# Attention units taken two at a time on the tensor engine, with a third buffer for the turned probabilities

## The reference

```
# even: 12 query heads of 64, 4 key heads, blocks of 128 queries, window of 128 to each side, a sink
p = exp(scores * HEAD_DIM**-0.5 - max);  out = p / (sum(p) + exp(sink - max)) @ v
# mix2: grouped: 8 query heads, 2 key heads, all 512 keys;  latent: 8 heads, keys of 64 + 32 (rotary), 512 keys
def one_block(qblk):                      # 128 queries
    sc = jnp.einsum('bqhgd,bkhd->bhgqk', qblk, k) * scale
    p = jax.nn.softmax(sc, axis=-1)
    return jnp.einsum('bhgqk,bkhd->bqhgd', p, v)
```

## Time and profile before

| | |
|---|---|
| time, median of 3 runs | 3439.11 us |
| span of the profiled execution | 3440.3 us |
| PE busy | 3396.7 us, 99% |
| DVE, POOL, ACT busy | 2088.8, 1993.6, 1529.6 us |
| attention of even | 440.2 to 506.9 us |
| attention of the first mix2 | 2074.9 to 2196.6 us |
| attention of the second mix2 | until 2927.3 us |

### The profile page before, as it was taken

One profiled execution on the slowest core, in us unless ns is written; L12 is line 12 of the kernel. 1 busy time (PEld: TensorE's weight loads), 2 busy tenths in 40 slices (PEclk: granted clock), 3 DMA queues, 4 the chain that ended last, 5 costly groups with the idle time before them and its releaser, 6 DMA issues.

```text
span 3440.3 us, 46280 instructions
## 1 busy us (share of the span) xinstructions
PE 3396.7 (99%) x17556; PEld 2760.0 (80%) x17556; DVE 2088.8 (61%) x2990; ACT 1529.6 (44%) x2388; POOL 1993.6 (58%) x2338
## 2 busy tenths in 40 slices
PE   9999999999999999999999999999999999999999
PEld 8888868888888888748888887788788877888887
DVE  5556766554764468766645657326766575238667
ACT  4334454333633354675333537434444545335444
POOL 6555655555655658735665557554655655546564
PEclk9999999999999999999999999999999999999999
DMA  4223303233222323202333220133222210232331
GB/s 173 93 75 115 110 18 123 74 110 111 88 97 96 125 71 94 69 1 83 123 111 107 79 75 26 50 98 123 98 98 88 90 59 8 92 104 92 115 107 62
DMA packets 89262, 303.59 MB, mean 88 GB/s; under 512 B 10448, under 2 KB 15056, under 8 KB 88656
## 3 DMA queue, kind: packets, MB, share of 16 engines
q1 hardware_dynamic: 86928, 298.53, 25.9%
q10 hardware_dynamic: 2112, 2.10, 0.2%
HBM read 296.39 MB, written 2.10 MB: 87 GB/s over the span
## 4 chain that ended last, share of the span: by engine, by line
PE 50%; DVE 5%; POOL 2%; issue 1%; ACT 1%; DMA 0%; DVEq 0%; POOLq 0%; ACTq 0%
PE bank L421 9%; PE bank L422 9%; PE bank L423 9%; PE bank L978 3%; PE bank L979 3%; PE bank L980 3%; PE bank L1295 2%; PE bank L1272 2%; PE scores L1257 2%; POOL extra_lo L410 2%; PE bank L2376 1%; PE bank L2377 1%; PE bank L2378 1%; DVE sqsum L579 1%; PE bank L1756 1%
## 5 line engine op out<-in xcount | busy, mean ns | idle before, releaser
L410 POOL TENSOR_TENSOR w_lo<-w_raw,w_hi 128x256 fp32r<-128x256 f32 x1754 | 1369.0, 814 | 1085.2 <-ACT w_hi L383 835.8
L421 PE MATMUL bank<-xh,w_hi 128*128 128x512 f32 x2544 | 997.0, 392 | 4.0 <-issue 1.5
L423 PE MATMUL bank<-xh,w_lo 128*128 128x512 f32 x2544 | 989.9, 389 | 0.0
L422 PE MATMUL bank<-xl,w_hi 128*128 128x512 f32 x2544 | 989.7, 389 | 0.0
L383 ACT ACTIVATE w_hi<-w_raw 128x1024 fp32r<-128x1024 f32 (+2 forms) x485 | 498.6, 1039 | 671.2 <-DMA w_raw<-in_ffn_up 269.4
L421 PEld LDWEIGHTS bank<-xh,w_hi 128*128 128x128 f32 x2544 | 478.5, 188 | 105.8 <-issue 4.1
L423 PEld LDWEIGHTS bank<-xh,w_lo 128*128 128x128 f32 x2544 | 478.3, 188 | 99.9
L422 PEld LDWEIGHTS bank<-xl,w_hi 128*128 128x128 f32 x2544 | 478.7, 188 | 98.0 <-issue 1.4
L410 POOL TENSOR_TENSOR extra_lo<-extra_raw,w_hi 128x256 fp32r<-128x256 f32 x264 | 229.7, 905 | 126.3 <-ACT w_hi L383 113.2
L1101 DVE TENSOR_TENSOR y_tok<-y_tok,bank 128x512 f32<-128x512 f32 x232 | 157.2, 684 | 223.1 <-PE bank L980 223.1
L1135 DVE TENSOR_TENSOR work<-bank,sqsum 128x512 f32<-128x512 f32 x88 | 60.6, 689 | 269.7 <-PE bank L423 269.7
(11 more groups left out here) (452 smaller groups left out, 6145.6 us busy)
## 6 DMA issues: line engine op xcount, KB each, us to landing
w_raw<-in_ffn_up SPq DMA_DIRECT2D x176, 512.0 KB, 3.5
w_raw<-in_b_ffn_up SPq DMA_DIRECT2D x64, 512.0 KB, 3.6
extra_raw<-in_ffn_down SPq DMA_DIRECT2D x52, 512.0 KB, 4.6
w_raw<-in_b_gates SPq DMA_DIRECT2D x48, 512.0 KB, 3.4
extra_raw<-in_b_ffn_down SPq DMA_DIRECT2D x40, 512.0 KB, 4.7
w_raw<-in_od_in SPq DMA_DIRECT2D x33, 512.0 KB, 3.7
w_raw<-in_b_in SPq DMA_DIRECT2D x24, 512.0 KB, 4.0
w_raw<-in_ffn_down SPq DMA_DIRECT2D x20, 512.0 KB, 3.4
```

The source lines that it names most:

```text
L410: ins = pool.tensor_tensor(lo_of(g, part), raw_of(g, part), hi_of(g, part).bitcast(F32), ALU.subtract)
L421: pe.matmul(out, wh, hi, start=first, stop=False)
L422: pe.matmul(out, wh, lo, start=False, stop=False)
L423: return pe.matmul(out, wl, hi, start=False, stop=last)
```

## The change

PE takes two units per step. Step k is: score(2k), score(2k+1), turn(2k-3), value(2k-5), value(2k-4), turn(2k-2). A joint now stands directly behind the passes of its own unit. The last value product of a call stands behind the second fill. `turned` has a third buffer, `turned_c`, laid over memory that is unused at that time, so the copies wait for the value product of unit g-3 and not g-2.

ACT takes per step: copy a(2k-3), exponentials(2k) and (2k+1) with their guests, copy a(2k-2), then the hi of 2k-5 or 2k-4. DVE keeps one unit per loop turn: maximum(s), reciprocal(s-1), then lo(s-7) (before: lo(s-5), behind the copy), then copy b(s-3). POOL, the DMA and the work of every station are unchanged.

```diff
-            for s in range(n + BEHIND + 1):
-                ...
+            for k in range(n // 2 + 3):
+                for s in (2 * k, 2 * k + 1):
+                    if s in early:
+                        early[s]()
+                    if s < n:
+                        score(s)
+                if 2 * k in fill:
+                    pe.wait_ge(probs_ready, c.units + n)
+                    fill[2 * k]()
+                if 0 <= 2 * k - 3 < n:
+                    turn(2 * k - 3)
+                if 0 <= 2 * k - 5 < n - 1:
+                    value(2 * k - 5)
+                if 0 <= 2 * k - 4 < n:
+                    value(2 * k - 4)
+                if 0 <= 2 * k - 2 < n:
+                    turn(2 * k - 2)
+                if 2 * k + 1 in fill:
+                    pe.wait_ge(probs_ready, c.units + n)
+                    fill[2 * k + 1]()
+                if 2 * k - 4 == n - 2:
+                    value(n - 1)
...
-                e = s - BEHIND - 2
+                e = s - 7
                 if 0 <= e < n and units[e]["n"] == 3:
...
+                if 0 <= s - 3 < n:
+                    u, g = units[s - 3], c.units + s - 3
+                    dve.wait_ge(turned_b, g + 1)
+                    if g >= 3:
+                        dve.wait_ge(attended, g - 2)
+                    dve.tensor_copy(turned[g % 3][:, 1, 0:u["keys"]], bank[TURNED + 1][:, 0:u["keys"]]).then_inc(copied_b, 1)
...
+            for k in range(n // 2 + 3):
+                if 0 <= 2 * k - 3 < n:
+                    copy(2 * k - 3)
+                for s in (2 * k, 2 * k + 1):
+                    if s < n:
+                        probs(s)
+                    if s in extra:
+                        extra[s]()
+                if 0 <= 2 * k - 2 < n:
+                    copy(2 * k - 2)
+                for s in (2 * k - 5, 2 * k - 4):
+                    if 0 <= s < n:
+                        head(s)
...
-        even_turned = [tmp, e_u[:, :, 0:S]]
+        even_turned = [tmp, e_u[:, :, 0:S], turned_c]
-        mix2_turned = [tmp, b_turned]
+        mix2_turned = [tmp, b_turned, turned_c]
```

More of the change, by code:

```diff
@@ L1237, in attend_pe @@
             n = len(units)
-            for s in range(n + BEHIND + 1):
-                if s in fill:
-                    pe.wait_ge(probs_ready, c.units + n)
[L1241 to L1298, removed]
@@ new lines, in score @@
+            def score(s):
+                u, g = units[s], c.units + s
+                if s == 2 and not early:
+                    idle_pe(pe, bank[HEADS[1]], 10)
+                if g >= 2:
+                    pe.wait_ge(probs_ready, g - 1)
+                if u["split"]:
+                    ready, many = u["split"]
+                    pe.wait_ge(ready, (SPLITS if ready is grouped_split else len(LATENTS)) * c.at("tables") + many)
+                last = len(u["passes"][0]) - 1
+                for p in range(last + 1):
+                    for side in range(2):
+                        query, key = u["passes"][side][p]
+                        mm = pe.matmul(scores[g % 2][:, side, 0:u["keys"]], query, key, start=u["opens"] and p == 0,
+                                       stop=u["closes"] and p == last, skip_group_check=True)
+                for side in range(2):
+                    for at, mask in u["masks"]:
+                        mm = pe.matmul(scores[g % 2][:, side, at:at + P], e_ident[:], e_mask[:, mask, :], start=False,
+                                       stop=True, skip_group_check=True)
+                if not u["joint"]:
+                    mm.then_inc(scores_ready, 1)
+                    return
+                pe.wait_ge(probs_ready, g)
+                for q, (query, key) in enumerate(u["joint"]):
+                    mm = pe.matmul(scores[(g + q // 2) % 2][:, q % 2, 0:u["keys"]], query, key, start=q >= 2, stop=q < 2,
+                                   skip_group_check=True)
+                    if q == 1:
+                        mm.then_inc(scores_ready, 1)
@@ new lines, in turn @@
+            def turn(s):
+                u, g = units[s], c.units + s
+                pe.wait_ge(probs_scaled, g + 1)
+                for side, (done, free) in enumerate(((turned_a, copied_a), (turned_b, copied_b))):
+                    if g:
+                        pe.wait_ge(free, g)
+                    for j in range(u["keys"] // P):
+                        mm = pe.transpose(bank[TURNED + side][:, j * P:(j + 1) * P],
+                                          pbuf[:, g % 4, side, j * P:(j + 1) * P], ident[:])
+                    mm.then_inc(done, 1)
@@ new lines, in value @@
+            def value(s):
+                u, g = units[s], c.units + s
+                pe.wait_ge(copied_a, g + 1)
+                pe.wait_ge(copied_b, g + 1)
+                hd = c.heads + u["head"]
+                if u["n"] == 0 and hd >= 2:
+                    pe.wait_ge(head_split, hd - 1)
+                if early and s in (0, 4):
+                    pe.wait_ge(vb_copied, 4 * c.at("tables") + (3 if s == 0 else 4))
+                many = u["keys"] // P
+                for j in range(many):
+                    for side in range(2):
+                        mm = pe.matmul(bank[HEADS[hd % 2]][side * HD:(side + 1) * HD, u["n"] * P:(u["n"] + 1) * P],
+                                       u["v"][side][j], turned[g % 3][:, side, j * P:(j + 1) * P],
+                                       start=j == 0, stop=j == many - 1, skip_group_check=True)
+                mm.then_inc(attended, 1)
@@ L1300, in attend_dve @@
         def attend_dve(dve, ch, c, units, turned, early=()):
             n = len(units)
-            for s in range(n + BEHIND + 3):
+            for s in range(n + 7):
                 if s in early:
```

58 lines of the change are left out of this document (25 added, 33 removed).

## The result

The changed kernel takes 3457.8 us (median of 4 runs, 3457.2 to 3460.0) against 3439.2 us of the kernel before beside it. The ratio is 1.0051, 95% interval 1.0037 to 1.0065, so it is 13 to 22 us slower; 3456.4 was forecast. The profiled span grew from 3440.3 to 3455.4 us.

The account below looks back on a forecast made before the run. PE, busy 99% of the span, was taken as the bound. Joins' savings and new waits net to +5.5 us in even and +5.9 in each mix2: 3439.1 + 17.3 = 3456.4 us, own range 3451 to 3462, stated range 3446 to 3464.

Parts of the forecast that it names:

- The joins: PE, all three attention calls: fewer changes of tile shape between neighbouring blocks save 7.6 us in all.
- third rival: Joins: V V, V T and T S keep their gaps, only the waits remain; 3460 us, chance 0.12.
- The steady chain: Grouped pairs: second score waits through turn, copy b, maximum, exponentials; 5.66 us a pair against 5.53 for PE alone.
- The start of mix2: First scores of mix2: S(5) waits 1.5 us for exponentials, the delay returns at later scores and turns; +4.0 us.
- The middle: Latent part of mix2: V(24) waits 2.0 us for lo(22), plus S(25), two joints, V(17), V(25); +4.4 us.
- The end: End of mix2: turn T(29) waits for copy a(28), which ACT does behind the exponentials of 31; +1.0 us.
- Even: Even's attention: four units take 9.70 us, not 9.05, with waits at scores, T(21) and the first fill; +5.5 us.
- The signs: Profile after: PE waits for ACT at every odd score, the forecast pair times and single waits appear, V V has no gap.
- DVE beside POOL: Small DVE products that meet a running POOL product end with it; 2.4 us of the total, mostly at the guests.
- no change: Rival: chains run as forecast but half of the single waits don't happen; 3443 us, chance 0.10.
- faster: Rival: copy b, maximum and exponentials fit in PE's step, so only the joins' saving is left; 3431.5 us, chance 0.05.
- clearly slower: Rival: steady steps lose 0.3 us more in each of the 44 pairs, +13 us; 3470 us, chance 0.08.

Follow-up runs that it names:

- lo early: Changed kernel with, on DVE, lo of both heads that end in a pair done in the first half of the step, ahead of copy b(2k-3): 3452.5 us.
- copy b twice: Changed kernel with DVE's copy b done twice, one behind the other: 3479.9 us, ratio 1.0113 to the kernel before.
- both maxima first: Changed kernel with DVE's order per pair altered so the second maximum, and both lo, go ahead of copy b(2k-3): 3452.2 us.
- last copy first: Changed kernel with ACT's copy a of the fourth unit from the end put ahead of the last unit's exponentials; run twice: 3461.2 and 3456.9 us.
- guests late: Changed kernel with the first four guests (rounding of latent operands on ACT, split on POOL) at units 6 to 9, not 2 to 5: 3458.0 us.
- spread kernel: Kernel before with only value products joined in mix2, three buffers, guests spread and one lo behind copy b; run twice: 3437.7 and 3437.2 us.

## Why the prediction held

- *The joins, -7.6 us.* V V is 1.90 us a pair of products (1.88 taken), V T and T S have the 0.17 of the other small gaps. The 0.16 us of V V, an extrapolation, was nearly right: 0.14. PE's busy time fell by 4.9 us, but its ends are modelled and the clock is in it, so the 7.6 as a whole was not measured. The third rival (the joins save nothing, 3460) is out by these rows; the time alone, 3457.8, lies between it and the forecast.
- *The steady chain.* 5.78 measured, 5.66 forecast, so 0.12 too little. The mis-sized term is the second score: I took 0.79 from its start to the turn, the value without a gap, but a score that has waited takes 0.90 (2115.61 - 2114.71). A wait takes back the join of two scores as well. The other terms of the chain held: 1.13 from turn to copy b, 0.61, and 3.12 from maximum to the next score (3.14 taken). Latent pairs: 6.81 measured (2132.18 to 2138.99), 6.80 forecast.
- *The start of mix2, 4.0.* From the first score of a pair to the turn behind the second, the pairs of scores 4, 6 and 8 take 3.37, 2.93 and 2.45 us in the timeline, where two scores without a wait take 1.59: 4.0 in all. The starts give S(5) 1.5, S(7) 1.0 and S(9) 0.8, and 0.3, 0.3 and 0.1 ahead of the turns behind them, of which 0.1 each is the score that had waited.
- *The middle, 4.4.* V(24) 2.0 (2.0), S(25) 0.7 (0.8), the joints 0.6 and 0.2 (0.65 and 0.35), V(17) and V(25) 0.3 and 0.3. Together 4.1. Run "lo early" took V(24)'s wait away alone.
- *The end, 1.0.* T(29) 0.9, and it was the copy, by the run that moved it, not POOL.
- *Even, +5.5.* +5.1, or +5.4 without the first two scores. Four units take 9.67 (474.82 to 484.49; 9.70 forecast), turn 21 waits 1.5 (1.5) and the first fill 1.5 for lo(19) (1.6).
- *The total.* Small errors cancel: V V and the chain cost a little more than forecast, the middle and even a little less. That a mix2 came at +5.9 to the tenth is in part luck. The median's +18.6 is above the stages' sum of 16.9; the mean granted clock was 0.997 in all four executions of the changed kernel, and 0.998 or 0.999 in 30 of 57 of the kernel before beside the experiments; what that is worth was not separated. The prediction put the profiled execution of before 1.2 us above the median by comparing its span with a time. In the changed kernel the span is 1.8 us less than the time of the same execution (3455.4 and 3457.2); by that estimate it was 3.0 us above, which fits its two falls of the clock.
- *The signs.* "PE waits at every odd score" came only in part: S(9) of even does not wait, and in the latent half, where a joint stands between the two scores, only S(25) does, for POOL's split.
- *DVE beside POOL.* The meetings are there: six small products of DVE in the first mix2 end with a product of POOL (last section), 4.3 us longer together than six of 0.17 us. Before there were six as well, 3.2 us longer. What they cost the whole wasn't tried, so the 2.4 us that the prediction gives them stays open.
- The rival "no change" needed half of the single waits to be missing; all came. The rival "faster" needed a chain under 5.53; it was 5.78. The rival "clearly slower" needed 0.3 us more in each pair; the latent pair came within 0.01.

Shown by runs: the chain through copy b (copy b twice, both maxima first), V(24) (lo early), T(21) and T(29) (last copy first), the buffer's neutrality. Read from the timeline but not tried one by one: the start's waits (only the guests were moved, and S(5)'s stayed), S(25), the joints, and even's fill.

## What to carry to other kernels

Before joining two producers that feed one double buffer, follow the chain from the second one back to itself through every engine: here the join saved 0.1 us in a pair and made the second score wait for the first one's consumers, since DVE stood in a copy that waited for the turn behind both scores. Join the stations that nobody waits for (here the value products) and leave the ones that start a chain apart. Waits that PE's order made could be mended here by the order on DVE and ACT, to a good half (8.7 us left of 18.6). A label "waited for X" or "issue" should be tested against what the waiting instruction needs, since the trace names whoever ended last before it, or nobody. And a gain has to be looked for where it arises: 0.9 of the 2.3 us that joined value products won in the first mix2 came from one product that moved ahead of a wait.

## What the runs showed of the hardware

- *A wait of PE can cost more than its length.* Behind the wait of V(24) the granted clock fell to 0.50 (1.2 GHz) in both mix2 of both profiles of "last copy first" and in the second mix2 of "copy b twice" (a wait of 2.6 us by the profile). It stayed at 1.00 in the first mix2 of "copy b twice" and in both mix2 of the changed kernel and of "guests late". A fall cost 1.7 us. Falls come elsewhere too, in some profiles and not in others: of these stretches outside the attention, the first two are the kernel before, the others the changed one, whose clock did not fall 5 us later either, where the same work stands.

```profile
546.00:554.00 8.00, 6.92 (x45) 6.57 (x45) 7.09 (x21) 4.89 (x14) 0.00 (x0) 0.81 0.21 66
1446.00:1454.00 8.00, 6.13 (x35) 5.17 (x36) 0.17 (x1) 4.86 (x11) 6.96 (x7) 0.79 0.13 33
```

```profile
546.00:554.00 8.00, 7.40 (x63) 7.22 (x62) 4.44 (x10) 2.30 (x6) 2.10 (x4) 1.00 0.25 72
1446.00:1454.00 8.00, 6.17 (x33) 4.58 (x32) 1.97 (x4) 7.30 (x13) 3.90 (x4) 1.00 0.22 71
```

 The start of even varies likewise: from 450 to 460 us the granted clock was 1.00 in after, 0.66 with both maxima first and 0.83 in the second profile of the spread kernel, whose even is the code of before; in its first profile, of the same program, it was 1.00. Most of the spread between executions (3436 to 3445 for the kernel before) goes with the mean granted clock (0.999 to 0.995). The Trainium skill (TensorE: Matmul & The Clock Gate, Part 1: The HAM clock gate) says that a gate sets the clock by how busy PE has been of late; that the falls at V(24) come behind an idle PE agrees. What decides whether the same wait draws one, no run here shows.
- *A small DVE product with a single input waits for POOL too.* I had put the meetings down to the two inputs of L1317. In the changed kernel the latent product L1339, which has one tensor and a constant and takes 0.17 us elsewhere, also ends with POOL's guest (2144.49 + 1.28 = 2145.77), while reductions and copies out of PSUM keep their 1.21 and 0.69 us beside POOL:

```profile
2144.49 1.28 POOL L2507 TENSOR_TENSOR qn_lo<-b_qn,hi_a 128x512 fp32r<-128x512 f32 x1
...
2144.84 0.95 DVE L1339 TENSOR_SCALAR red<-red 128x2 f32<-128x2 f32 x1
```

 The Trainium skill (GPSIMD Engine Reference, Specifications) names, beside two SBUF inputs, a 2-port performance mode of DVE; whether L1339 runs in it no run here shows.
